# Query and key projections with 512-column products, adaLN slices in other places, filler products in some waits

## The chip, the cores and the metric

The kernel runs on one core of one Trainium2 chip. The metric is the device time of one execution in microseconds (us), here the median of three timed runs: 604.17 us (602.7 to 604.27). One further execution was recorded by the hardware profiler, and all rows below come from it.

## The reference

One layer of a decoder block in float32 on x of 256 rows (tokens) by 1024 channels, with a conditioning vector c:

```python
mod = silu(c) @ ada_w + ada_b                      # six rows of 1024: shift, scale, gate; twice
u = modulate(rms_norm(x, norm_mix_g), sh_a, sc_a)
proj = u @ w_in                                    # q_m k_m v_m o_m if_m | q_a k_a v_a | g_m g_a
...                                                # mLSTM on q_m k_m v_m; windowed attention on q_a k_a v_a (12 heads of 128)
y = sigmoid(g_m) * (h_m @ w_branch_m) + sigmoid(g_a) * (h_a @ w_branch_a)
x = x + gt_a * (y @ w_out)
u = modulate(rms_norm(x, norm_ffn_g), sh_f, sc_f)
x = x + gt_f * moe(u, ...)                         # 16 experts, two per token
return rms_norm(x, final_norm_g)
```

w_in alone is 1024 by 10760 numbers. q_a and k_a take 1536 of its columns each.

## The kernel before

**Precision.** Each weight tile and each activation is split into a high part in fp32r (a reduced float32 that TensorE multiplies in one pass) and a low part, the rest. A product of both is taken as three: high weight by high u, high weight by low u, low weight by high u, all summed in one PSUM bank (L1573 to L1577, L1595 to L1599).

**Blocks.** The projection weights are cut into groups of 512 columns (`GROUP_LIST`): four `qk`, two `vm`, three `qa` (groups 6 to 8), three `ka` (9 to 11), three `va` (12 to 14), two `o`, two `gm`, two `ga`, then the branch and output projections (`bm`, `ba`, `wo`). A block is half a group: 512 of the 1024 rows of its weights, 1 MB. The `qa` and `ka` groups are blocks 12 to 23, in pairs: an even block begins a group, the odd one ends it. In a channel-major group (`qk`, `qa`, `ka`, gates, branches) the weights are the stationary operand: for each of 4 column tiles c and 4 row tiles k there are three products of 256 moving columns (the 256 tokens). In the other groups u is stationary and the weights stream, 512 columns at a time.

**Pipeline.** SP loads blocks into four `raw` tiles, in the order of `STREAM`, and starts a load when the item four places ahead of it in that order is used up. For block s, the loop of ScalarE (ACT) makes the high part of block s+2 (`split_hi`, L613, one copy of 128x2048), VectorE (DVE) makes its low part (`split_lo`, L953), and TensorE (PE) multiplies block s. Each engine takes its instructions in the order in which they are written.

**Banks.** A group sums in two banks, 0 and 1 or 2 and 3, in turn (`banks_of`). For `qa` and `ka` ACT copies both banks out in one go when the group's second block is done (L721), and the group after next waits for that (`evacuated`, before its first product).

**adaLN slices.** The four later rows of `mod` are summed on DVE from 16 slices of `ada_w` of 1 MB each (`ada`, L982), which go through the same `raw` tiles. `ADA_AT` says in which block's loop turn each stands: 12, 13, 14, 15, 17, 18, 19, 21, 22, 23, 25, 26, 27, 30, 33, 36. A slice stands behind that turn's `split_lo` and ahead of its attention work on DVE.

**Between the blocks** PE does the mLSTM (a score after blocks 14, 16, 18, 20, L1645 to L1649; the values after 15, 17, 19, 21, L1662; small transposes after 12 and 13) and the attention (scores after 28, 31, 34, 37, turns after 30, 33, 36, 39, values after 31, 34, 37, 40).

**mod_p.** Behind block 41 ACT copies two rows of `mod` into `mod_p` (L782) once all 16 slices are summed, with one event for both. PE turns the first row into columns behind block 42 and the second behind block 43 (L1718).

**Routing.** After the last projection PE makes the router logits, DVE ranks experts and tokens (`picked`, `rank0`), and builds `onehot` for both token tiles t (L1340), with one signal at the end. PE then gathers the rows of the first experts (L1776). ACT rounds these rows (`xg_hi`), DVE makes their low part (`xg_lo`, L1330). In waits of this part PE also starts the sums of the output (`start_sums`, L1750) and does one product whose result nobody reads (L1758).

**Experts.** Eight pairs of experts follow (L1788 gate and up, L1800 and L1810 down). Their weights come through a ring of 19 chunks of 1 MB; SP loads the next chunk when one is used (L469).

## Time and profile before

| | us |
|---|---|
| median of the timed runs | 604.17 (602.7, 604.17, 604.27) |
| the profiled execution | 600.97 |
| its span, first to last instruction | 599.1 |
| PE busy | 577.4 (96%) |
| DVE busy | 306.9 (51%) |
| ACT busy | 238.7 (40%) |
| granted TensorE clock, mean | 0.997 |

The page first gives the busy time of each engine, then 40 slices of the span (busy tenths of each engine, granted clock, DMA), then the chain of work that ended last: followed back from the end, at each step to what released it. A busy time is an average over stages; what a change in one stage is worth is read in that stage, from what the chain passes through. The span leaves 1.87 us of the profiled execution's own time around it.

### The profile page before, as it was taken

The page shows a single profiled execution, that of the slowest core. Times are in us where ns is not written, and L with a number is a line of the kernel's source. Part 1 is how long each engine was busy: PE and PEld are TensorE (multiplying, and loading weights), DVE is VectorE, ACT ScalarE, POOL GpSimd, SP SyncE. Part 2 cuts the span into 40 slices and gives each one's busy share as a digit, 9 for nine tenths or more (in the row PEclk, how much of TensorE's full clock was granted, in tenths as well). Part 3 has the DMA queues.
Part 4 walks back from the last instruction along what each step waited for, and adds up shares of the span by engine and source line. Part 5 has one row for each costly group of instructions (what it writes and reads, how often), then busy time and mean ns, then how long its engine had stood idle before and what let it go on. Part 6 is the DMA issues. An engine that isn't in the chain of part 4 may idle for free.

```text
span 599.1 us, 8462 instructions
## 1 busy us (share of the span) xinstructions
PE 577.4 (96%) x3563; PEld 423.3 (71%) x3563; DVE 306.9 (51%) x461; ACT 238.7 (40%) x330; POOL 9.0 (2%) x23
## 2 busy tenths in 40 slices
PE   3999999999999999999999999999999999999995
PEld 0789988999998888999999988533534444353432
DVE  0679976766568966677546683712212130221204
ACT  5617658444454545764683334701111020111113
POOL 3001000000000000000000000000000000000000
PEclk9999999999999999999999999999999999999998
DMA  8999664785859947636558989399999999999992
GB/s 309 387 332 323 212 206 140 282 287 209 287 209 341 328 170 279 220 107 237 198 217 318 416 341 357 154 378 423 421 419 422 423 421 419 422 421 422 421 382 78
DMA packets 51577, 184.78 MB, mean 308 GB/s; under 512 B 3649, under 2 KB 3761, under 8 KB 37713
## 3 DMA queue, kind: packets, MB, share of 16 engines
q1 hardware_dynamic: 50706, 183.53, 79.7%
q8 instruction: 29, 0.48, 0.3%
q10 hardware_dynamic: 704, 0.58, 0.3%
q0 software_dynamic: 128, 0.11, 0.1%
q14 instruction: 10, 0.08, 0.0%
HBM read 183.16 MB, written 1.05 MB: 307 GB/s over the span
## 4 chain that ended last, share of the span: by engine, by line
PE 90%; DVE 3%; ACT 3%; DMA 1%; issue 1%; SPq 0%; ACTq 0%; DVEq 0%
PE ps L1576 30%; PE ps L1788 18%; PE ps L1598 16%; PE ps L1800 8%; PE ps L1834 3%; PE ps L1776 2%; DMA first_ada<-in_ada_w_dram 1%; PE ps L1810 1%; PE ps L1683 1%; PE ps L1698 1%; PE ps L1662 1%; PE ps L1494 1%; PE ps L1827 1%; DVE lo L953 1%; PE ps L1587 1%
## 5 line engine op out<-in xcount | busy, mean ns | idle before, releaser
L953 DVE TENSOR_TENSOR lo<-raw,hi 128x2048 fp32r<-128x2048 f32 (+1 forms) x51 | 114.2, 2248 | 41.2 <-ACT hi L613 40.8
L1576 PE MATMUL ps<-u_hi,hi 128*128 128x256 f32 x416 | 120.3, 289 | 0.7 <-DVE lo L953 0.7
L1576 PE MATMUL ps<-u_lo,hi 128*128 128x256 f32 x416 | 117.9, 283 | 0.0
L1576 PE MATMUL ps<-u_hi,lo 128*128 128x256 f32 x416 | 117.9, 283 | 0.0
L1788 PE MATMUL ps<-ring,xe_t 128*64 128x512 f32 x512 | 111.7, 593 | 0.0
L613 ACT CAST hi<-raw 128x2048 fp32r<-128x2048 f32 x50 | 94.9, 1908 | 36.0 <-PE ps L1576 25.5
L1788 PEld LDWEIGHTS ps<-ring,xe_t 128*64 128x64 f32 x512 | 36.5, 137 | 71.7 <-issue 71.4
L1576 PEld LDWEIGHTS ps<-u_hi,hi 128*128 128x128 f32 x416 | 79.8, 192 | 2.1 <-DVE lo L953 1.1
L1576 PEld LDWEIGHTS ps<-u_lo,hi 128*128 128x128 f32 x416 | 79.9, 192 | 0.2
L1576 PEld LDWEIGHTS ps<-u_hi,lo 128*128 128x128 f32 x416 | 79.9, 192 | 0.0
L1800 PE MATMUL ps<-ring,he_t 128*64 128x512 f32 x224 | 49.6, 596 | 0.0
L1399 DVE SCALAR_TENSOR_TENSOR he<-ps,w_slot,sg 128x512 f32<-128x512 f32 x8 | 6.0, 750 | 82.6 <-PE ps L1788 82.6
L1598 PE MATMUL ps<-hi,u_hi 128*128 128x512 f32 x112 | 44.4, 396 | 0.0
L1598 PE MATMUL ps<-lo,u_hi 128*128 128x512 f32 x112 | 43.7, 390 | 0.0
L1598 PE MATMUL ps<-hi,u_lo 128*128 128x512 f32 x112 | 43.7, 390 | 0.0
L1381 DVE TENSOR_TENSOR y_e<-ps,mod 128x512 f32<-128x512 f32 x16 | 10.4, 687 | 54.5 <-PE ps L1800 47.8
L982 DVE SCALAR_TENSOR_TENSOR mod<-raw,cs,mod 128x2048 f32<-128x2048 f32 x16 | 37.5, 2346 | 0.0
L1800 PEld LDWEIGHTS ps<-ring,he_t 128*64 128x64 f32 x224 | 15.5, 137 | 30.2 <-issue 28.0
L867 ACT CAST y_hi_e<-y_e 128x512 fp32r<-128x512 f32 x16 | 9.8, 618 | 62.8 <-DVE y_e L1381 62.8
L861 ACT COPY he_t<-ps 128x512 f32<-128x512 f32 x8 | 4.7, 586 | 64.3 <-PE ps L1827 64.3
L1598 PEld LDWEIGHTS ps<-lo,u_hi 128*128 128x128 f32 x112 | 21.0, 188 | 4.5
L1598 PEld LDWEIGHTS ps<-hi,u_hi 128*128 128x128 f32 x112 | 21.1, 188 | 4.2
(334 smaller groups left out, 837.0 us busy)
## 6 DMA issues: line engine op xcount, KB each, us to landing
raw<-in_w_in_dram SPq DMA_DIRECT2D x41, 1024.0 KB, 5.2
ring<-in_w_gate_e_dram SPq DMA_DIRECT2D x32, 1024.0 KB, 17.4
ring<-in_w_up_e_dram SPq DMA_DIRECT2D x32, 1024.0 KB, 16.0
ring<-in_w_down_e_dram SPq DMA_DIRECT2D x28, 1024.0 KB, 16.0
raw<-in_ada_w_dram SPq DMA_DIRECT2D x16, 1024.0 KB, 5.3
first_ada<-in_ada_w_dram SPq DMA_DIRECT2D x16, 512.0 KB, 11.8
raw<-in_w_branch_m_dram SPq DMA_DIRECT2D x4, 1024.0 KB, 5.5
raw<-in_w_out_dram SPq DMA_DIRECT2D x4, 1024.0 KB, 6.1
```

The lines of the kernel that those rows point to most:

```text
L613: nc.scalar.copy(hi[b % RING][:], src[:]).then_inc(hi_ready, 1)
L867: nc.scalar.copy(y_hi_e[:, h * NB:(h + 1) * NB], y_e[:, h * NB:(h + 1) * NB]).then_inc(y_hi_ready, 1)
L953: ins = V.tensor_tensor(lo[b % RING][:, tiles, :], src[:, tiles, :], hi[b % RING][:, tiles, :].bitcast(F32), ALU.subtract)
L982: V.scalar_tensor_tensor(out=dst, in0=src[:].rearrange("p k n -> p (k n)"), scalar=cs[:, k:k + 1], in1=dst, op0=ALU.mult, op1=ALU.add).the ...
L1381: ins = V.tensor_tensor(y_e[:, h * NB:(h + 1) * NB], ps[6 + h][:], mod[:, 3, h * NB:(h + 1) * NB], ALU.mult)
L1399: V.scalar_tensor_tensor(out=he[:], in0=ps[5][:], scalar=w_slot[:, side:side + 1], in1=sg[:], op0=ALU.mult, op1=ALU.mult).then_inc(he_read ...
L1576: ins = mm(dst, w[:, k, cols], x[:, k0 + k, :], start=(first and c % 2 == 0 and k == 0 and n == 0), stop=(end and k == KB - 1 and n == 2), ...
L1598: ins = mm(ps[banks[t]][:], x[:, k0 + k, rows_t], w[:, k, :], start=(first and k == 0 and n == 0), stop=(end and k == KB - 1 and n == 2))
L1776: ins = mm(dst, x[:, t, kk * P:(kk + 1) * P], onehot[:, t, 0:cols], start=(part == 0 and kk % 2 == 0 and t == 0), stop=(part == 1 and t == ...
L1788: ins = mm(ps[bank][64 * s:64 * s + 64, :], xe_t[:, kk, col + s * SLOTS:col + (s + 1) * SLOTS], w[:, k, :], start=(kk == 0), stop=(kk == K ...
L1800: ins = mm(ps[6 + h][64 * s:64 * s + 64, :], he_t[:, kk, s * SLOTS:(s + 1) * SLOTS], w[:, k, h * NB:(h + 1) * NB], start=(kk == 0), stop=( ...
L1834: ins = mm(ps[2 * t + h][:], scat[side][:, t * P:(t + 1) * P], y[:, h * NB:(h + 1) * NB], start=False, stop=False, skip_group_check=True)
```

## The change

1. **`qa` and `ka`.** The high and low part of u become two halves of one tile (`u_both`). For each c and k one product of 512 moving columns (high weight by both parts of u) takes the place of two of 256; the sum with the low part lands in the right half of the bank. The third product (low weight by high u) is as before. Each column tile c has a bank of its own, so a group takes four banks (2, 3, 0, 1) and the next group the same four.
2. **Getting the result out.** For each pair of banks ACT copies the right halves to `q_a` or `k_a` (`copy_right`), and DVE adds the left halves (`add_halves`). In a group's last block, ACT's copies for the first pair stand ahead of its `split_hi`, those for the second pair behind it, and DVE's sums likewise around its `split_lo`. PE waits for a pair's sum before it writes that pair in the next group (`wide_free`).
3. **adaLN slices** in loop turns 12, 14, 16, 18, 20, 22, 25, 26, 27, 29, 30, 32, 33, 36, 38, 39. As places, 13, 15, 17, 19, 21 and 23 are given up and 16, 20, 29, 32, 38 and 39 are taken.
4. **`mod_p`** has an event for each of its rows, and PE waits for the row it needs.
5. **Filler products**: eight of 256 columns ahead of block 3, five of 256 ahead of the last transposes of the routing, four (instead of one) ahead of `picked`.
6. **Routing order**: `start_sums(0, 0)` goes ahead of the wait for the last logits; `onehot` gives a signal after its first tile, and the first four gather products take the tiles in that order.

```diff
-ADA_AT = {s: ADA_FIRST + i for i, s in enumerate([12, 13, 14, 15, 17, 18, 19, 21, 22, 23, 25, 26, 27, 30, 33, 36])}
+ADA_AT = {s: ADA_FIRST + i for i, s in enumerate([12, 14, 16, 18, 20, 22, 25, 26, 27, 29, 30, 32, 33, 36, 38, 39])}
...
+            def copy_right(g, pair):
+                for c in (2 * pair, 2 * pair + 1):
+                    ins = nc.scalar.copy(wide_out(g, c), ps[wide_banks(g)[c]][:, T:2 * T])
+                ins.then_inc(halved, 1)
             for s in range(NBLK):
+                g, _, _, end = BLOCKS[s]
+                if end and g in WIDE:
...
+                    act.wait_ge(pair_done, WIDE.index(g) + 1)
+                    copy_right(g, 0)
                 if s + AHEAD < NBLK and s + AHEAD != EARLY and s != LAST_BLOCK[24]:
                     split_hi(s + AHEAD)
+                if end and g in WIDE:
+                    act.wait_ge(block_done, s + 1)
+                    copy_right(g, 1)
...
                     for m in range(2):
-                        ins = nc.scalar.copy(dealt(mod_p[:, m, :]), nearby(mod[:, 1 + m, :]))
-                    event(ins, "mod_p")
+                        event(nc.scalar.copy(dealt(mod_p[:, m, :]), nearby(mod[:, 1 + m, :])), f"mod_p{m}")
...
+            def add_halves(g, pair):
+                dve.wait_ge(halved, 2 * WIDE.index(g) + pair + 1)
+                for c in (2 * pair, 2 * pair + 1):
+                    ins = V.tensor_tensor(wide_out(g, c), ps[wide_banks(g)[c]][:, 0:T], wide_out(g, c), ALU.add)
+                ins.then_inc(summed, 1)
...
+                if end and g in WIDE:
+                    add_halves(g, 0)
                 if s + AHEAD < NBLK and s not in (1, LAST_BLOCK[24]):
                     split_lo(s + AHEAD)
+                if end and g in WIDE:
+                    add_halves(g, 1)
...
-            ins.then_inc(onehot_ready, 1)
+                ins.then_inc(onehot_ready if t else onehot_first, 1)
...
+            def keep_busy(bank, count, left, right):
+                for _ in range(count):
+                    mm(ps[bank][:, 0:T], left, right, start=True, stop=True)
...
-                if first and g >= EARLY:
-                    evacuated(pe, g - EARLY if g < EARLY + 2 else g - 2)
+                if first and g >= EARLY and g not in WIDE:
+                    if g - 1 in WIDE:
+                        wide_free(pe, g - 1, 0)
+                    else:
+                        evacuated(pe, g - EARLY if g < EARLY + 2 else g - 2)
...
+                if s == EARLY:
+                    keep_busy(6, 8, u_hi[:, 0, 0:P], u_hi[:, 0, :])
...
+                elif g in WIDE:
+                    for c in range(4):
+                        bank = wide_banks(g)[c]
+                        if first and c % 2 == 0:
+                            if g - 1 in WIDE:
+                                wide_free(pe, g - 1, c // 2)
+                            else:
+                                evacuated(pe, g - 2 + c // 2)
+                        cols = slice(c * P, (c + 1) * P)
+                        for k in range(KB):
+                            mm(ps[bank][:].rearrange("p (a t) -> p a t", a=2), w_hi[:, k, cols], u_both[:, :, k0 + k, :],
+                               start=(first and k == 0), stop=False, skip_group_check=True)
+                            ins = mm(ps[bank][:, 0:T], w_lo[:, k, cols], u_hi[:, k0 + k, :], start=False,
+                                     stop=(end and k == KB - 1), skip_group_check=True)
+                        if end and c == 1:
+                            ins.then_inc(pair_done, 1)
...
-                    after(pe, "mod_p", "a_turned3")
                     m = FFN_COL_AT.index(s)
+                    after(pe, f"mod_p{m}", "a_turned3")
...
             event(logits(0, 1), "logits0")
+            keep_busy(1, 5, y_hi[:, 0, 0:P], y_hi[:, 0, :])
             after(pe, "x1_1_t1_0", "x1_1_t1_1")
...
             event(ins, "x1_turn1_t1")
+            start_sums(0, 0)
             after(pe, "x1_copied1_t1", "x1_turned1_t1")
             event(logits(1, 1), "logits1")
...
             evacuated(pe, 26)
-            start_sums(0, 0)
-            for _ in range(1):
-                mm(ps[3][:, 0:T], ident[:], mod[:, 0, 0:T], start=True, stop=True)
+            keep_busy(3, 4, ident[:], mod[:, 0, 0:T])
             after(pe, "picked")
...
             after(pe, "xg_hi0_0", "xg_hi1_0")
-            pe.wait_ge(onehot_ready, 1)
-            gather_part(0, 4 * SLOTS, 4, (0,))
+            for t in range(TT):
+                pe.wait_ge(onehot_ready if t else onehot_first, 1)
+                for kk in range(2):
+                    mm(ps[4][:, kk * T:(kk + 1) * T], xg_hi[:, t, kk * P:(kk + 1) * P], onehot[:, t, :],
+                       start=(kk == 0 and t == 0), stop=False, skip_group_check=True)
```

## Rows read from the trace of the kernel before

**Rows 1.** The page: busy us, share of the span and instructions of each engine.

```profile
PE 577.4 (96%) x3563; PEld 423.3 (71%) x3563; DVE 306.9 (51%) x461; ACT 238.7 (40%) x330; POOL 9.0 (2%) x23
```

**Rows 2.** Chain that ended last, in order of time: start us, us, what.

```profile
112.59 0.21 PE ps L1633 x2
...
142.49 5.75 PE ps L1576 x48
...
155.93 1.30 PE ps L1662 x6
...
212.68 10.93 PE ps L1598 x48
...
410.30 13.73 PE ps L1788 x64
```

**Rows 3.** Waits of the SP queue: in total, times, longest.

```profile
SPq L469 <- PE ps L1788: 69.0, 26, 13.3
```

**Rows 4.** Timeline of ACT, blocks 17 and 18: start, duration, operation, idle before.

```profile
136.80 1.89 ACT L613 CAST hi<-raw 128x2048 fp32r<-128x2048 f32 x1
...
142.58 0.38 ACT L744 COPY h_m<-ps 128x256 f32<-128x256 f32 x1
```

**Rows 5.** Timeline of DVE: blocks 17 and 18, and one row of the last projection.

```profile
138.72 2.29 DVE L953 TENSOR_TENSOR lo<-raw,hi 128x2048 fp32r<-128x2048 f32 x1 [1.23 <-ACT hi L613]
140.93 2.35 DVE L982 SCALAR_TENSOR_TENSOR mod<-raw,cs,mod 128x2048 f32<-128x2048 f32 x1
...
372.27 0.42 DVE L1135 TENSOR_TENSOR scratch<-ps,mod 128x256 f32<-128x256 f32 x1
```

**Rows 6.** Timeline of DVE during attention, first instructions behind blocks 31 and 40.

```profile
234.03 0.42 DVE L1228 SCALAR_TENSOR_TENSOR bias_a<-dist,masks 128x256 f32<-128x256 f32 x1 [3.53 <-PE ps L1698]
...
300.50 1.66 DVE L1255 SCALAR_TENSOR_TENSOR hm_lo<-ps,vec,hm_hi 128x256 fp32r<-128x256 f32 x4 [4.83 <-ACT hm_hi L772]
```

**Rows 7.** The page: DMA issues, KB each, median us to landing.

```profile
raw<-in_ada_w_dram SPq DMA_DIRECT2D x16, 1024.0 KB, 5.3
```

**Rows 8.** Timeline of PE: first product of block 3, and mod_p.

```profile
45.06 0.39 PE L1557 MATMUL ps<-u_hi,hi 128*128 128x256 f32 x1 [0.94 <-DVE u_lo L1030]
...
312.13 1.95 PE L1718 MATMUL ps<-ones,mod_p 128*128 128x1 f32 x16 [0.89 <-ACT mod_p L782]
```

**Rows 9.** Timeline of ACT: both copies of mod_p.

```profile
307.98 4.10 ACT L782 COPY mod_p<-mod 128x1024 f32<-128x1024 f32 x2
```

**Rows 10.** Timeline of all engines during the routing.

```profile
373.29 0.72 PE L1743 MATMUL ps<-ident,x_res 128*128 128x128 f32 x4 [0.41 <-DVE rt L1282]
...
374.60 1.06 PE L1530 MATMUL ps<-rw_scaled,x_res_t 128*128 128x16 f32 x8 [0.59 <-DVE x_res_t L1289]
...
374.86 1.28 ACT L830 ACT_TABLE_LOAD   x1
...
377.31 1.02 PE L1750 MATMUL ps<-x_res,ident 128*128 128x512 f32 x2
...
378.17 0.60 PE L1758 MATMUL ps<-mod,ident 128*128 128x256 f32 x2
...
379.05 1.15 DVE L1330 SCALAR_TENSOR_TENSOR xg_lo<-x_res,st,xg_hi 128x512 fp32r<-128x512 f32 x1
379.18 0.41 PE L1762 MATMUL ps<-rt,bias_a 128*128 128x32 f32 x2 [0.42 <-DVE rt L1322]
...
380.32 0.76 DVE L1340 TENSOR_TENSOR onehot<-bias_a,rt 128x256 fp32r<-128x256 f32 x2
...
381.08 1.13 DVE L1330 SCALAR_TENSOR_TENSOR xg_lo<-x_res,st,xg_hi 128x512 fp32r<-128x512 f32 x1
...
382.27 1.21 PE L1776 MATMUL ps<-onehot,xg_lo 128*128 128x256 f32 x8
```

**Rows 11.** Stretches: us, busy time by engine, granted clock, DMA share, GB/s.

```profile
374.00:382.00 8.00, 6.75 (x31) 4.10 (x31) 6.19 (x29) 7.48 (x10) 0.00 (x0) 1.00 0.74 309
...
595.00:599.10 4.10, 0.00 (x0) 0.00 (x0) 0.90 (x2) 0.72 (x1) 0.00 (x0) 0.56 0.68 256
```

More of the change, by code:

```diff
@@ L69 @@
 AHEAD = RING - 1
+WIDE = [_g for _g, (_kind, _, _) in enumerate(GROUP_LIST) if _kind in ("qa", "ka")]
 CONV_AT = {3: (0, 0), 4: (0, 1), 5: (1, 0), 6: (1, 1), 7: (2, 0), 8: (3, 0), 9: (3, 1), 10: (2, 1)}
@@ L158, in build @@
         lo = [at(f"lo{i}", 56 + 8 * i, [P, KB, NB], F32R) for i in range(RING)]
-        u_hi = at("u_hi", 80, [P, KT, T], F32R)
-        u_lo = at("u_lo", 88, [P, KT, T], F32R)
+        u_both = at("u_both", 80, [P, 2, KT, T], F32R)
+        u_hi, u_lo = u_both[:, 0], u_both[:, 1]
         hm_hi = at("hm_hi", 80, [P, KT, T], F32R)
@@ L281, in build @@
         xe_early = sem("xe_early")
+        onehot_first = sem("onehot_first")
         onehot_ready, slots_turned, gathered, xe_act, xe_dve, scat_ready, scattered = (sem(n) for n in (
@@ L348, in plan @@
                 if s == M_TURN_AT[1]:
-                    act += ["ha_hi", "mod_p"]; dve.append("ha_lo")
+                    act += ["ha_hi", "mod_p0", "mod_p1"]; dve.append("ha_lo")
                 if s == FFN_COL_AT[1]:
@@ L400, in evac_engine @@
         def evac_engine(g):
+            if GROUP_LIST[g][0] in ("qa", "ka"):
+                return "sums"
             return "dve" if GROUP_LIST[g][0] in ("qk", "bm", "ba", "wo") else "act"
@@ L406, in banks_of, with wide_banks, wide_out, wide_free @@
             return 2 * n, 2 * n + 1
+        def wide_banks(g):
+            return 2, 3, 0, 1
+        def wide_out(g, c):
+            kind = GROUP_LIST[g][0]
+            j = [x for x in WIDE if GROUP_LIST[x][0] == kind].index(g)
+            return {"qa": q_a, "ka": k_a}[kind][:, 4 * j + c, :]
+        def wide_free(eng, g, pair):
+            eng.wait_ge(summed, 2 * WIDE.index(g) + pair + 1)
         def evacuated(eng, g):
+            if g in WIDE:
+                wide_free(eng, g, 1)
+                return
             e = evac_engine(g)
@@ L706, in _ @@
                         after(act, "m_val3")
-                    if kind == "qa" and j == 0:
-                        after(act, "u_lo1_3")
                     if kind == "va" and j == 0:
                         after(act, "m_val3")
-                    dst = {"va": v_a, "o": sig_o, "qa": q_a, "ka": k_a, "gm": sig_gm, "ga": sig_ga}.get(kind)
+                    dst = {"va": v_a, "o": sig_o, "gm": sig_gm, "ga": sig_ga}.get(kind)
                     for n, bank in enumerate(banks):
@@ L1046, in _ @@
             ada(4)
+            def add_halves(g, pair):
[3 more added lines that the diff above has]
+                ins.then_inc(summed, 1)
             for s in range(NBLK):
+                g, _, _, end = BLOCKS[s]
+                if end and g in WIDE:
+                    add_halves(g, 0)
                 if s + AHEAD < NBLK and s not in (1, LAST_BLOCK[24]):
                     split_lo(s + AHEAD)
+                if end and g in WIDE:
+                    add_halves(g, 1)
                 if s == 0:
@@ L1744, in _, with start_sums @@
             event(ins, "x1_turn1_t1")
+            def start_sums(t, h):
+                mm(ps[2 * t + h][:], ident[:], x_res[:, t, h * NB:(h + 1) * NB], start=True, stop=False, skip_group_check=True)
+            start_sums(0, 0)
             after(pe, "x1_copied1_t1", "x1_turned1_t1")
             event(logits(1, 1), "logits1")
-            def start_sums(t, h):
-                mm(ps[2 * t + h][:], ident[:], x_res[:, t, h * NB:(h + 1) * NB], start=True, stop=False, skip_group_check=True)
             for n in range(2):
```

3 lines of the change are left out of this document (added).

## The prediction

> **What bounds the kernel now.** I read the busy times first: PE is busy for 577.4 of 599.1 us and no other engine for more than 51% [rows 1]. Such a share doesn't say that PE sets the time in every stage, so I read the chain of waits next. The reader should see that in the blocks it runs from PE product to PE product without a gap [rows 2], that it leaves PE only around mod_p (0.89 us of waiting [rows 8]) and in the routing (waits of 0.41, 0.59 and 0.42 us [rows 10]), and that the experts are again PE alone. The SP queue's waits come third: the experts' loads wait for PE (69.0 us for L1788 alone [rows 3]), so a start of the experts that is earlier by some time brings their loads forward by the same time. What PE saves ahead of the experts should therefore arrive whole at the end; a transfer doesn't swallow it. Last come ACT and DVE in the same blocks, because the change gives them more to do between two products.
>
> **Part 1, the products.** 48 products of 256 columns take 5.75 us, so 0.1198 us each; 48 of 512 take 10.93 us, so 0.2277 each [rows 2]. Twice the columns cost 0.108 us more, so some 0.012 us of each product doesn't depend on its columns. Before, one column tile c and row tile k cost 3 x 0.1198 = 0.3594 us; after it costs 0.2277 + 0.1198 = 0.3475, which is 0.0119 less. There are 12 blocks x 16 of them, 192, so -2.3 us, all of it PE time on the chain. No row shows a product whose moving columns come as two strips of 256, nor the two lengths in turn, so I bound it: if the strips cost what two products cost, the gain is 0 (a loss would need a strip dearer than a product of its own, for which no row speaks); if 512 columns cost as little as in the experts' products (13.73 us for 64, 0.2145 each [rows 2]) and 256 half of that, a tile costs 0.322 and the gain is 7.2 us. I take 2.3, since the rows with the same kind of number and the same stationary size give it.
>
> By the Trainium skill (TensorE: Matmul & The Clock Gate, Back-to-back issue gap) a product costs its columns at 2.4 GHz plus 2.5 ns, so joining two saves only 2.5 ns, an estimated 0.5 us over 192. The rows show about 12 ns, so I go by the rows; the rule's outcome is a rival below.
>
> **Part 1, getting results out.** A wide block takes 16 x 0.3475 = 5.56 us. Call its start B. The first pair of banks is done at B+2.78. ACT then copies two halves: 0.38 us each [rows 4], so about B+3.5; DVE adds two, 0.42 each for this size [rows 5], so about B+4.3. PE needs that pair at the next group's start, B+5.56 or later: 1.2 us to spare. Queued behind ACT's wait for the pair are its split of block s+2 (1.89 us [rows 4]) and everything after it; it now ends at about B+5.4, and DVE's low part (2.29 us [rows 5]) at B+7.7. PE wants that low part a whole block and more later, so no cost. Then the second pair: copied at about B+6.3, but its sums stand behind DVE's low part, so B+8.5. PE wants this pair in the middle of the next group's first block: B+5.56, plus the work between the blocks, plus 2.78. That work is 1.30 us for the values behind blocks 15, 17, 19 and 21 [rows 2], so B+9.6 and 1.1 us to spare; behind block 13 it is only 0.21 us [rows 2], so B+8.55 and nothing to spare. Behind block 23 no wide group follows, and group 12 needs the first pair at once, when DVE and ACT have just done the mLSTM's scale: another place with little cover. I take 0.2 us for both, bounds 0 and 2. The old copies of `qa` and `ka` and their waits go at no gain: the chain holds no wait for them.
>
> **Part 3, the slices.** The six places given up are exactly the turns with the new sums. That takes 6 x 2.3 = 14 us off DVE there and the two new places, 16 and 20, put 4.6 back; six of the ten slices of this stretch stay, all in even turns. If all ten had stayed, one slice of 2.35 us [rows 5] would stand ahead of several second-pair sums that have 1.1 us or less to spare. So this move gains nothing by itself; it pays for part 1. The four taken later (29, 32, 38, 39) fall on DVE time during the attention: DVE idles 3.53 us ahead of its work on the scores of block 31 (block 34's is alike, of the two rows one stands), and 4.83 us ahead of the turns of block 40 [rows 6]. One slice of 2.27 us of queue fits in each of the first two; 38 and 39 together, 4.5 us, fit in the last. Each also brings its load on the SP queue: 1 MB that lands after 5.3 us [rows 7], in one of four tiles, so the weight block behind it is asked for one item later and ACT may get it 2 to 3 us later than before. PE wants a block about two blocks (11 us) after its load, so this is covered. The cost is 0; if that cover is gone, one slice, 2.3 us, at one place.
>
> **Part 4.** mod_p's two copies run from 307.98 for 4.10 us [rows 9]; the first ends at about 310.0. PE starts on the first row at 312.13 after 0.89 us of waiting [rows 8], so it was free at 311.24. With an event for each row it goes on at once, and the second row is ready long before block 43 ends: -0.9 us, bounds -1.0 and 0. The last slice, now in turn 39, falls into DVE's idle time that ends at 300.50 [rows 6], ahead of 307.98.
>
> **Part 5, filler products.** Ahead of block 3 PE waits 0.94 us [rows 8]; eight products of 0.12 us fill it: 0, at most +0.1. Five ahead of the last transposes (0.6 us) fill a wait of 0.41 [rows 10]: up to +0.2. Four ahead of `picked`: `start_sums(0, 0)`, which took 0.86 us of PE's queue (377.31 to 378.17), leaves this place, and three more products come; one of 256 columns in float32 takes 0.60 us to its end alone and about half of the 0.86 of one of 512 in a row, 0.43. So +0.4 us against a wait of 0.42 [rows 10]: 0 to +0.2. The granted clock is 1.00 through the routing [rows 11], so in this execution there is nothing to win with them.
>
> **Part 6.** `start_sums(0, 0)` takes 0.86 us in a wait of 0.59, so the last logits come 0.3 us later; the sigmoid after them waits for ACT's table load anyway (374.86 to 376.14 [rows 10]), which hides 0.2 of it. The split signal lets PE gather 0.38 us earlier (half of 0.76), but the low-part products start at 382.27, and DVE's second low part ends at 382.21 [rows 10]: the time is lost in the next wait. Parts 5 and 6 together: +0.1, bounds -0.2 and +0.6.
>
> **The sum.** -2.3 + 0.2 - 0.9 + 0.1 = -2.9 us. The profiled execution took 600.97 us, so 598.1 in its terms. The timed runs took 602.7 to 604.27, 1.7 to 3.3 us more than the profiled one, which no row explains; I carry the difference over unchanged: 604.17 - 2.9 = 601.3 us, 0.5% less. A measurement of this kernel can tell about 0.3% (1.8 us) from no change.
>
> **The rivals.**
>
> *The joined product saves nothing.* Two strips cost what two products cost. For it: no row shows strips. Against: both lengths carry the same 12 to 14 ns. Part 4 alone is left: 604.17 - 0.9 + 0.3 = about 603.6. By the Trainium skill's rule above it would be 603.1, an estimate, within this rival's reach and part of its chance.
>
> *Waits take the gain.* The new bank waits cost 0.4 us at each of five borders between wide groups: -2.9 + 2.0, 603.3. For it: one set of four banks instead of two in turn, and no spare time behind block 13. Against: 1.1 us at four borders.
>
> *Slower: DVE becomes the bound in blocks 12 to 23.* Its queue holds split, slice, mLSTM score and four sums for each group; if its second-pair sums come 2.7 us later than counted (one slice or split more ahead of them), PE waits 1.6 us at four borders and 2.7 at one: +9.1, so about 610. It decides from 1.9 us of lateness on, where the waits (4 x 0.8 + 1.9 = 5.1) pass 2.9 + 1.8 and the 0.2 counted. Against: DVE idles here, 1.23 us ahead of one split [rows 5].
>
> *The filler products win what the profile can't show.* The clock does fall when PE has nothing to do: 0.56 granted in the last 4.1 us [rows 11], that is 1.2 GHz for most of it. If the 1.7 to 3.3 us by which the timed runs are longer are such stretches in the waits that are now filled, they go too: 598 to 599.6. The Trainium skill (TensorE: Matmul & The Clock Gate, Part 1) says that the slow clock is the default and activity releases it. The trace agrees at its end, and shows no fall in the waits concerned.
>
> **How the numbers follow.** Forecast 0.58, products save nothing 0.07, waits take the gain 0.13, slower 0.08, filler products win 0.14. The forecast's own bounds are 600.0 to 602.6, so most but not all of it counts as faster. Faster: 0.50 of the forecast, and 0.14: 0.64. Within 0.3%: the rest of the forecast, both middle rivals: 0.28. Slower: 0.08. The range leaves out the slower rival and the far half of the last one: 598.7 to 603.7.
>
> **What would show it.** Right: PE blocks 12 to 23 at about 5.56 us each with 16 products of 512 and 16 of 256; no PE wait for DVE's sums over 0.2 us; no wait ahead of L1718; the routing within 0.3 us of 373.3 to 382.3 in length; the same pitch in the experts. Wrong: a tile of 0.36 us for the first rival; PE waits named after the add lines at each border for the second and third; a fall of the granted clock somewhere in a profile for the last. The forecast fails most easily where DVE's order in the odd turns is later than I counted.

## The result

| | before | after |
|---|---|---|
| timed runs, median (range) | 604.16 us (602.7 to 604.27, 4 runs) | 597.67 us (597.18 to 598.16, 4 runs) |
| ratio after/before, 95% interval | | 0.9906 [0.9881, 0.9931] |
| profiled execution: time, span | 600.97, 599.1 | 597.18, 595.4 |
| start of the first block's products | 23.08 | 22.43 |
| first of the gates' running sums, ahead of block 12 | 100.05 | 99.39 |
| start of block 24 | 183.32 | 180.61 |
| start of the `mod_p` products | 312.13 | 308.40 |
| start of the experts' products | 384.37 | 380.62 |

The change gained 6.5 us; I had predicted 2.9. The two profiled executions differ by 3.7 to 3.8 us only. So two things are to be explained: the 3.7, and the other 2.8.

**The 3.7 us between the traces.** The table's differences from row to row are what each stage gained: 0.65 before the first block, in work that the change doesn't touch; 2.05 in blocks 12 to 23; 1.05 around `mod_p` (312.13 to 308.40 is 3.73 earlier, block 24 was 2.71 earlier, and the stages between lost 0.03); after that nothing, for the start of the experts is 3.75 earlier and the end 3.7. The 0.65 are scatter and no gain: in the fourteen traces without idle products at the start (those of the experiments below among them) the first block starts at 22.10 to 23.22 us, early or late with either kernel (22.21 in e3, which is the kernel before but for eight products; 23.22 in e14, which is nearly the kernel after). So some 3.1 us are the change's. First the busy times of after, from the page, for [rows 1]:

```profile
PE 577.1 (97%) x3390; PEld 414.3 (70%) x3390; DVE 315.2 (53%) x485; ACT 240.3 (40%) x342; POOL 9.0 (2%) x23
```

PE's busy sum hardly moved (577.4 before), since the idle products (the filler products of the change) count as busy; a sum over the span would have hidden both gains. Then the chain that ended last (start us, us, what), whose rows answer [rows 2, 8]:

```profile
119.19 0.45 PE ps L1721 x4
125.18 1.30 PE ps L1734 x6
...
180.77 27.24 PE ps L1670 x120
...
302.81 5.76 PE ps L1648 x48
308.56 1.68 PE ps L1790 x16
```

Block 15 begins at 119.19 + 0.45 = 119.64 and ends at 125.18: 5.54 us where a block took 5.75. `mod_p` (L1790, the old L1718) follows the block before it without a gap. And two column-and-row tiles of the new form, in PE's timeline of after:

```profile
123.97 0.40 PE L1625 MATMUL ps<-u_both,hi 128*128 128x512 f32 x1
124.20 0.28 PE L1627 MATMUL ps<-u_both,lo 128*128 128x256 f32 x1
124.32 0.39 PE L1625 MATMUL ps<-u_both,hi 128*128 128x512 f32 x1
124.55 0.27 PE L1627 MATMUL ps<-u_both,lo 128*128 128x256 f32 x1
124.67 0.40 PE L1625 MATMUL ps<-u_both,hi 128*128 128x512 f32 x1
```

From 123.97 to 124.67 two tiles: 0.35 each, where the sum had 0.3475. Between 100 and 184 us the trace of after lists no wait of PE. The loads of the experts wait for PE as before (waits of the SP queue, for [rows 3]):

```profile
SPq L491 <- PE ps L1860: 70.3, 26, 13.4
```

In the routing the timeline of PE, for [rows 10], has the idle products where waits were, and the one wait that is left stands where the sum had put it, ahead of the low-part products:

```profile
368.90 0.84 PE L1576 MATMUL ps<-y_hi 128*128 128x256 f32 x5
369.58 0.65 PE L1816 MATMUL ps<-ident,x_res 128*128 128x128 f32 x4
370.06 1.02 PE L1820 MATMUL ps<-x_res,ident 128*128 128x512 f32 x2
...
378.52 1.22 PE L1848 MATMUL ps<-onehot,xg_lo 128*128 128x256 f32 x8 [0.17 <-DVE xg_lo L1376]
```

**The other 2.8 us** are not in these two traces. The expectations below go by two theories. The one is that part of before's executions lose granted TensorE clock behind short waits (a fall, below: a stretch at a granted clock of 0.50), which the idle products and the halved `mod_p` take away. The rival is that products, slices and `mod_p` are worth more than the traces show, or that the chips and moments differ.

### The profile page after: what moved, and what is told of

It reads as the page before. It is cut to its first block, busy times and chain, and to the rows that moved or that the text cites. A ratio compares the mean times of both kernels' runs of the same rounds, so it can differ in the third digit from the quotient of the medians.

```text
span 595.4 us, 8152 instructions
## 1 busy us (share of the span) xinstructions
PE 577.1 (97%) x3390; PEld 414.3 (70%) x3390; DVE 315.2 (53%) x485; ACT 240.3 (40%) x342; POOL 9.0 (2%) x23
## 3 DMA queue, kind: packets, MB, share of 16 engines
HBM read 183.16 MB, written 1.05 MB: 309 GB/s over the span
## 4 chain that ended last, share of the span: by engine, by line
PE 92%; DVE 3%; ACT 2%; DMA 1%; issue 1%; SPq 0%; ACTq 0%; DVEq 0%
PE ps L1648 20%; PE ps L1860 19%; PE ps L1670 16%; PE ps L1872 8%; PE ps L1625 8%; PE ps L1627 4%; PE ps L1906 3%; PE ps L1848 2%; DMA first_ada<-in_ada_w_dram 1%; PE ps L1882 1%; PE ps L1659 1%; PE ps L1770 1%; PE ps L1755 1%; PE ps L1734 1%; PE ps L1540 1%; PE ps L1899 1%
## 5 line engine op out<-in xcount | busy, mean ns | idle before, releaser
L1648 PE MATMUL ps<-u_both,hi 128*128 128x256 f32 x448 | 82.1, 285 | 0.7 <-DVE lo L987 0.7
L1648 PEld LDWEIGHTS ps<-u_both,hi 128*128 128x128 f32 x448 | 69.8, 191 | 2.1 <-DVE lo L987 1.1
L1670 PE MATMUL ps<-hi,u_both 128*128 128x512 f32 x224 | 69.8, 393 | 0.0
L1625 PE MATMUL ps<-u_both,hi 128*128 128x512 f32 x192 | 68.8, 401 | 0.0
L1648 PE MATMUL ps<-u_both,lo 128*128 128x256 f32 x224 | 63.4, 283 | 0.0
L1627 PE MATMUL ps<-u_both,lo 128*128 128x256 f32 x192 | 53.7, 279 | 0.0
L1670 PEld LDWEIGHTS ps<-hi,u_both 128*128 128x128 f32 x224 | 41.7, 188 | 8.5
L1670 PE MATMUL ps<-lo,u_both 128*128 128x512 f32 x112 | 43.7, 390 | 0.0
L1648 PEld LDWEIGHTS ps<-u_both,lo 128*128 128x128 f32 x224 | 42.9, 191 | 0.0
L1625 PEld LDWEIGHTS ps<-u_both,hi 128*128 128x128 f32 x192 | 36.0, 188 | 8.0
L1627 PEld LDWEIGHTS ps<-u_both,lo 128*128 128x128 f32 x192 | 36.2, 189 | 0.1
```

The costliest lines, as they stand in the source:

```text
L1625: mm(ps[bank][:].rearrange("p (a t) -> p a t", a=2), w_hi[:, k, cols], u_both[:, :, k0 + k, :], start=(first and k == 0), stop=False, skip ...
L1627: ins = mm(ps[bank][:, 0:T], w_lo[:, k, cols], u_hi[:, k0 + k, :], start=False, stop=(end and k == KB - 1), skip_group_check=True)
L1648: ins = mm(dst, w[:, k, cols], x[:, k0 + k, :], start=(first and c % 2 == 0 and k == 0 and n == 0), stop=(end and k == KB - 1 and n == 2), ...
L1670: ins = mm(ps[banks[t]][:], x[:, k0 + k, rows_t], w[:, k, :], start=(first and k == 0 and n == 0), stop=(end and k == KB - 1 and n == 2))
```

## The experiments

Each was timed beside the kernel before on its own chip. "Clock" is the mean granted clock of an execution; before's trace has 0.997 without any fall but that of the last microseconds, where PE has no work [rows 11].

**The kernel before, seen often.** The experiments below hold 81 further executions of it, in five sets on four chips. By their mean clock they come in three groups:

| mean clock | executions | median us | range |
|---|---|---|---|
| 0.995 to 0.997 | 44 | 601.3 | 600.7 to 601.7 |
| 0.991 to 0.992 | 27 | 602.8 | 602.5 to 603.2 |
| 0.987 to 0.990 | 10 | 604.5 | 604.2 to 606.1 |

The profiled execution (600.97) belongs to the first group; of the four by which the change was judged, by their times, three lie at 604.2, in the last, and one in the second. That was an unusual draw: the last group holds 10 of the 81, and the median of all 81 is 601.5 us, so that after (597.6 over ten executions) is 3.9 us below it, and not 6.5. The two slower groups make up from 3 of 13 to 9 of 17 executions, by set; whether the sets differ by chance or by something of the chip isn't shown. None of the ten executions of after (597.0 to 598.4) has a clock below 0.996.

The mean clock also holds the end of the span, where PE has no work: there the traces stand at 0.50 for 1.5 to 4.6 us, which costs nothing and takes 0.001 to 0.004 off the mean. Between 0.995 and 0.997 it therefore doesn't tell whether there was a fall: e2's and e8's traces, at 0.995, hold one behind a wait, after's, at 0.996, none. The first group isn't shown to be free of falls; the 37 executions at 0.992 or less lost more than the end accounts for in any trace.

**Without the idle products.**

```diff
# kernel after
-                if s == EARLY:
-                    keep_busy(6, 8, u_hi[:, 0, 0:P], u_hi[:, 0, :])
...
-            keep_busy(1, 5, y_hi[:, 0, 0:P], y_hi[:, 0, :])
...
-            keep_busy(3, 4, ident[:], mod[:, 0, 0:T])
+            keep_busy(3, 1, ident[:], mod[:, 0, 0:T])
```

> The changed kernel without the filler products (none ahead of block 3 and of the last transposes, one ahead of picked as before). Theory A (the fillers keep TensorE's clock from falling in runs that the one profile of before doesn't show): about 600.5 us, that is 597.7 plus most of the 1.7 to 3.3 us by which the timed runs of before were longer than its profiled one. Theory B (the products, mod_p and the order make the whole gain, the fillers nothing): 597.7 within 0.4. Either way blocks 12 to 23 gain 2.05 us and the wait ahead of mod_p is gone.

Measured: 598.37 us (596.89 to 599.07, 6 runs), ratio to before 0.9945 [0.9928, 0.9962]; its trace has no fall ahead of the last microseconds and a span of 595.1. The time lies between the two theories: most of the gain stands without idle products, and they are worth at most about 0.8 us here.

**Idle products and the moved `start_sums` on the kernel before.**

```diff
# kernel before
+                if s == EARLY:
+                    keep_busy(6, 8, u_hi[:, 0, 0:P], u_hi[:, 0, :])
...
+            keep_busy(1, 5, y_hi[:, 0, 0:P], y_hi[:, 0, :])
...
+            start_sums(0, 0)
             after(pe, "x1_copied1_t1", "x1_turned1_t1")
...
-            start_sums(0, 0)
-            for _ in range(1):
-                mm(ps[3][:, 0:T], ident[:], mod[:, 0, 0:T], start=True, stop=True)
+            keep_busy(3, 4, ident[:], mod[:, 0, 0:T])
```

> The kernel before with the filler products alone and the earlier start_sums(0, 0) that makes room for them. Theory A: about 601 us (604.2 less 1.7 to 3.3), close to the profiled 600.97. Theory B: 604.2 within 0.4, perhaps 0.1 to 0.2 longer.

Measured: 601.76 us (600.82 to 602.77, 12 runs), ratio 0.9994 [0.9977, 1.0011]. The executions with a clock of 0.992 or less are gone. The median is 0.9 us below that of the 23 executions of before beside it (602.67), but the interval of the ratio holds no change, and the lowest times (600.82 and 600.72) are the same. The trace shows why there is no more: a fall in a place that no idle product covers. Stretches, with the columns of [rows 11]:

```profile
313.60:317.60 4.00, 4.00 (x23) 4.00 (x22) 4.00 (x2) 1.31 (x1) 0.00 (x0) 0.57 0.38 81
374.00:382.00 8.00, 7.74 (x37) 4.89 (x36) 5.51 (x31) 7.34 (x12) 0.00 (x0) 1.00 0.81 316
```

This is block 43, right behind the wait for `mod_p` and its sixteen one-column products: 23 products in 4 us, where the trace of before has 35 from 314 to 318. The routing is at full clock.

**Only the eight early ones; only `start_sums`.** e3 is before with the first of these edits, e4 with the third:

```diff
# e3
+                if s == EARLY:
+                    keep_busy(6, 8, u_hi[:, 0, 0:P], u_hi[:, 0, :])
# e4
+            start_sums(0, 0)
             after(pe, "x1_copied1_t1", "x1_turned1_t1")
...
-            start_sums(0, 0)
```

> The kernel before with the eight fillers ahead of block 3 alone. Theory A if the clock falls there: about 601 us. Theory A if it falls in the routing: 604.2. Theory B: 604.2.

> The kernel before with start_sums(0, 0) moved ahead of the wait for the last logits, and nothing else. In the runs so far 12 of 23 executions of before had a mean granted clock of 0.992 or less and spans of 601 to 604 us, the others 0.995 to 0.997 and 599.0 to 599.7; with all late fillers none of 12 fell. Theory A1 (filling the wait of 0.59 us is enough to keep the clock): no execution at 0.992 or less, median about 601.2 us. Theory A2 (the filler products are needed): about half of the executions at 0.992 or less, median 602 to 603. Its own price: 0 to +0.2 us.

Measured: e3 603.27 us (600.85 to 604.67), ratio 1.0015 [0.9997, 1.0032]; e4 603.70 us (601.12 to 604.97), ratio 1.0021 [1.0005, 1.0037]; 12 runs each. Neither holds the clock: eight of e3's executions stand at 0.992 or less, and eleven of e4's, though e4 moves only 0.86 us of work. The traces name the places. The stretches of e4:

```profile
45.00:50.00 5.00, 5.00 (x31) 5.00 (x31) 4.90 (x10) 5.00 (x6) 1.65 (x3) 0.66 0.99 312
314.80:318.40 3.60, 3.60 (x20) 3.60 (x19) 3.60 (x2) 1.45 (x1) 0.00 (x0) 0.53 0.39 88
382.80:386.40 3.60, 3.35 (x15) 3.13 (x15) 3.60 (x8) 1.22 (x2) 0.00 (x0) 0.54 0.00 0
```

Three places: block 3 behind its wait of 0.94 us, block 43 behind `mod_p`'s, the gather behind the routing's waits. In e4's timeline of PE one sees the pitch of the products of 256 columns double:

```profile
312.70 1.95 PE L1718 MATMUL ps<-ones,mod_p 128*128 128x1 f32 x16 [0.89 <-ACT mod_p L782]
...
314.71 0.33 PE L1576 MATMUL ps<-hm_lo,hi 128*128 128x256 f32 x1
314.84 0.41 PE L1576 MATMUL ps<-hm_hi,lo 128*128 128x256 f32 x1
315.06 0.42 PE L1576 MATMUL ps<-hm_hi,hi 128*128 128x256 f32 x1
315.27 0.41 PE L1576 MATMUL ps<-hm_lo,hi 128*128 128x256 f32 x1
```

0.21 us from start to start instead of 0.12: 1.2 instead of 2.4 GHz. Against the trace of before, this stage (first `mod_p` product to first product of the last projection) took 35.89 instead of 34.39 us, so a fall here costs 1.5 us. In e3's trace block 3 is at full clock, and two falls are left: one behind `mod_p`, whose stage takes 35.88 us, and one of 7 us in the routing, which takes 20.23 instead of 17.60. They account for the whole time: 599.1 (the span of before's trace), less 0.87 for a first block that starts at 22.21, plus 1.5 and 2.6 is 602.3, and e3's span is 602.4.

**After, without idle products and with `start_sums` in its old place.**

```diff
# e1, and
-            start_sums(0, 0)
             after(pe, "x1_copied1_t1", "x1_turned1_t1")
...
             evacuated(pe, 26)
+            start_sums(0, 0)
```

> The changed kernel with the routing's waits as before: no filler products, start_sums(0, 0) in its old place with one filler. Theory A1 or A2 (it is the work in these waits that keeps the clock): about half of the executions at a granted clock of 0.992 or less, times of 597, 599 and 600.5 us, median some 1.5 us over the changed kernel's 597.7. Theory A3 (the clock is kept by the earlier end of the blocks, not by these waits): none falls, median about 597.3.

Measured: 598.84 us (597.97 to 599.74, 6 runs), ratio 0.9949 [0.9934, 0.9964]. The falls are back in two of the three places (45 to 48.6 at 0.55, 372.8 to 376.4 at 0.53 in its trace, span 598.0), and not behind `mod_p`, whose halves this kernel keeps.

**The old slices in after.**

```diff
# kernel after
-ADA_AT = {... [12, 14, 16, 18, 20, 22, 25, 26, 27, 29, 30, 32, 33, 36, 38, 39])}
+ADA_AT = {... [12, 13, 14, 15, 17, 18, 19, 21, 22, 23, 25, 26, 27, 30, 33, 36])}
```

> The changed kernel with the adaLN slices where they were before (10 in blocks 12 to 23, none in 16, 20, 29, 32, 38, 39). My step on the slices: the second-pair sums come late, PE waits 1 to 2 us more in all at the borders of the wide groups, so 598.7 to 599.7 us, and blocks 12 to 23 keep 0 to 1 us of their gain. Rival (DVE had room for all): 597.7 within 0.4, and no PE wait for the sums.

Measured: 598.37 us (598.0 to 599.2, 6 runs), a little below the expected 598.7 to 599.7, ratio 0.9945 [0.9931, 0.9958], at a clock of 0.998 or 0.999. Blocks 12 to 23 take 82.36 us in its trace, 1.14 more than in after; the waits of PE between 100 and 184 us (total, times, longest) show part of it, and after shows none:

```profile
PE ps L1625 <- DVE q_a L1086: 0.4, 1, 0.4
PE ps L1734 <- DVE turned L1251: 0.2, 1, 0.2
```

So the slices' move gains by itself what the old order would have cost the new sums: 1.1 of the 2.05 us, of which 0.6 is in waits that the view names.

**Everything but the new products and slices.** e2 with `mod_p` in two halves.

```diff
# e2, and
-                        ins = nc.scalar.copy(dealt(mod_p[:, m, :]), nearby(mod[:, 1 + m, :]))
-                    event(ins, "mod_p")
+                        event(nc.scalar.copy(dealt(mod_p[:, m, :]), nearby(mod[:, 1 + m, :])), f"mod_p{m}")
...
-                    after(pe, "mod_p", "a_turned3")
+                    after(pe, f"mod_p{m}", "a_turned3")
```

> The kernel before with all idle products, start_sums in its new place and mod_p in two halves; products and slices stay old. By the theory that three places lose granted clock in part of the executions, and that the two halves of mod_p mend the one behind the modulation (about 313 to 318 us), no place is left: 600.8 (the best executions of e2) less 1.05 for the shorter wait is 599.7, with every execution within 0.8 us of it, median 599.7 to 600.2. Kernel after less this one is then what products and slices are worth, 2.0 to 2.5 us. Rival: the fall behind the modulation does not hang on the length of that wait; then part of the executions still lose 1.5 us there, the median is 600.6 or more and the spread is over 1.5 us.

Measured: 599.49 us (598.76 to 600.43, 6 runs), ratio 0.9957 [0.9944, 0.9971], no fall in the trace ahead of the last microseconds and every execution at 0.997 or 0.998. This is the first theory's outcome, with small misses: the median is 0.2 us under its range, one execution 0.9 from 599.7, and the spread of 1.7 us would fit the rival; but the rival's median (600.6 or more) and its fall are not there. After (597.6 over ten executions) is 1.9 us below this, for products and slices, where 2.0 to 2.5 were expected.

**`mod_p` in two halves, alone on the kernel before:** the edit just shown, without e2.

> The kernel before with mod_p in two halves and nothing else. By the theory of three places every execution gains 1.05 us, and those that lost 1.5 us behind the modulation gain that too; the falls at 45 to 50 us and in the routing stay in part of the executions: best executions at 599.5 to 600.2, median 600.0 to 601.5, a profile that shows no fall from 310 to 320 us. Rival: that fall stays; then its profile or a group of executions 1.5 us longer shows it, and the median is 1.0 us below before's and no more.

Measured: 600.74 us (598.77 to 602.75, 12 runs), ratio 0.9966 [0.9943, 0.9988]. The twelve lie in three bunches: 598.8 to 599.0, 600.3 to 601.1, 602.4 to 602.8. The lowest lies under the range expected for it (599.5 to 600.2) and 2.4 us under the first group of before on the same chip (601.1 to 601.6), though the halves gain 1.06 us in the trace (from block 24 to `mod_p` it takes 127.75 us, in before's 128.81). An execution of before with a first block at 22.10 and no fall would have a span of 599.1 - 0.98 = 598.1, and the shortest of the 81 has 599.0; so that first group seems to lose about 1 us more to late starts or to falls of its own, and which it is no trace shows. e13's trace:

```profile
309.00:317.00 8.00, 8.00 (x70) 8.00 (x69) 4.09 (x3) 6.68 (x4) 0.00 (x0) 1.00 0.76 304
373.60:380.40 6.80, 6.80 (x15) 3.70 (x16) 3.91 (x22) 5.43 (x8) 0.00 (x0) 0.50 0.82 325
```

No fall behind `mod_p`, a long one in the routing. What that costs, in its timeline of PE (the four products of `mod` by ones took 1.96 us in the trace of before):

```profile
373.44 1.70 PE L1529 MATMUL ps<-rw_scaled,x_res_t 128*128 128x16 f32 x8 [0.59 <-DVE x_res_t L1288]
374.98 3.76 PE L1752 MATMUL ps<-mod,ones 128*128 128x512 f32 x4
378.53 1.92 PE L1749 MATMUL ps<-x_res,ident 128*128 128x512 f32 x2
```

The routing, from the first product of the logits to the first of the experts, takes 20.26 us in this trace and 17.60 in that of before: 2.7 us for one fall. The shorter one of e5 makes it 18.59 against 17.68 in after, 0.9, and that of e4 18.90 against 17.60, 1.3.

**Which idle products matter.** Each is after less one or two of its idle products:

```diff
# e8
-                if s == EARLY:
-                    keep_busy(6, 8, u_hi[:, 0, 0:P], u_hi[:, 0, :])
# e9, e14
-            keep_busy(1, 5, y_hi[:, 0, 0:P], y_hi[:, 0, :])
# e14
-            keep_busy(3, 4, ident[:], mod[:, 0, 0:T])
+            keep_busy(3, 1, ident[:], mod[:, 0, 0:T])
```

> The kernel after without the eight idle products ahead of block 3. By the theory of three places, the stretch from 45 to 50 us falls to half the clock in part of the executions, which adds 0.9 us to those: 597.2 to 599, median 597.5 to 598.5, with two groups of spans. Rival: the fall of e4 and e5 at 45 to 50 us came with start_sums in its old or lone place, or by chance, and not from this wait; then all executions stand as those of after, and eight products of 1 us in all cost or save nothing over 0.2 us.

> The kernel after without the five idle products on the attention output in the routing (the four on the scratch bank and the eight early ones stay). If these five hold the clock through the routing, part of the executions fall to half the clock somewhere from 368 to 385 us, which adds 1 to 2.6 us: some of 599 or more. Rival: the four ahead of the experts, or start_sums in its new place, are enough: all executions within 0.6 us of after.

> The kernel after with only the eight early idle products (none in the routing but the one that the kernel before had). e1, without any, was 0.7 us above after, and e8, without the eight alone, 0.7 too. If the eight early ones are all that pays, this is after again: 597.2 to 598.2, no execution below a clock of 0.995. Rival: the late ones hold the clock in the routing: part of the executions lose 1 us or more there, some of 599 or more.

Measured: e8 598.38 us (598.0 to 598.8, 5 runs), ratio 0.9940 [0.9926, 0.9955]; e9 597.77 (597.09 to 598.18, 6 runs), 0.9932 [0.9919, 0.9945]; e14 597.13 (596.92 to 598.83, 6 runs), 0.9912 [0.9886, 0.9938]. e8's trace has the fall ahead of the value blocks:

```profile
45.00:48.60 3.60, 3.60 (x20) 3.60 (x20) 3.50 (x9) 3.60 (x6) 1.65 (x3) 0.55 1.08 383
```

From the first product of block 0 to the first of L1670 (512 columns) it takes 52.35 us, after 51.48: 0.87 us. Of its five executions that one alone stands at 0.995, though; the other four, at 0.997, are between 596.3 and 596.8 in span, with no trace. And e1's trace, without the eight too, has the wait of 0.94 us ahead of block 3 and no fall: it takes 51.48 us, as after. e9 and e14 show no fall in their traces and stand with after, but for one execution of e14 at 598.83. So in the kernel after, with `start_sums` moved and `mod_p` halved, the idle products in the routing buy nothing that these runs show; the eight early ones cost nothing, and the fall that costs 0.9 us was seen there only without them (e4, e5, e8), in part of the executions.

**After once more.** The same kernel as after.

> The kernel after itself once more, beside more executions of the kernel before on the same chip. The kernel before took 601.5 to 602.7 us in the larger sets of e1 to e10 and 604.2 in the two small sets by which the change was judged. If that gap is the share of executions of before that lose granted clock, after stays at 597.2 to 598.2 with a clock of 0.995 or more each time, and the difference lies between 3.5 us (against executions of before without a fall) and 6.5 us. Rival: the chips or the moments differ; then after moves with before, by 2 us or more.

Measured: 597.53 us (597.02 to 598.36, 6 runs); before on the same chip 602.61 (601.08 to 605.94, 17 runs); ratio 0.9916 [0.9891, 0.9941]. After stayed where it was, before spread over its three groups. The difference, 5.1 us, lies in the first theory's 3.5 to 6.5, and after didn't move with before, as the rival had it.

**Idle products at the start.** The 0.65 us before the first block lie in products of the same work: sixteen transposes took 2.46 us in before and 1.97 in after, and the first eight products 1.94 in both where later ones take 1.06. Such slow products at the start come and go from execution to execution (in the trace of e14, whose edit lies in the routing, the transposes take 2.74). e10 adds fourteen idle products of 128 columns at the very start of after, e12 eighteen; e15 adds twenty-four, and five between the first two groups; e16 is e15 with e14's edit.

```diff
# kernel after (e15)
+            for _ in range(24):
+                mm(ps[1][:, 0:P], ident[:], ident[:], start=True, stop=True)
             pe.wait_ge(rows_loaded, 80)
...
                 row_sums(0, 2, a, a == 0, False)
+                if a == 0:
+                    for _ in range(5):
+                        mm(ps[1][:, 0:P], ident[:], ident[:], start=True, stop=True)
```

> The kernel after with fourteen more idle products, of 128 columns, at the very start, where the matrix engine has nothing to do for 9.7 us and its first products then take 1.94 us for eight where the same form later takes half. If these first products are slow because the granted clock is still low, and idle products raise it sooner, the stage up to the first block (start at 22.4 us) is 0.3 to 0.9 us shorter: median 596.7 to 597.4. Rival: the chain there is set by the input's transfers, which land at about 12 us, or the clock comes up no sooner: within 0.2 us of after.

> Like e10, with eighteen instead of fourteen idle products at the start, so that the matrix engine is busy to about 9.5 us and goes on without the idle 2.1 us behind which e10 fell to half the clock. If that idle time made the fall, the first eight products take about 1.06 us instead of 1.93 and the first block starts 0.3 to 0.8 us earlier than at 22.1 to 22.4: median 596.9 to 597.5. Rival: the products run past 9.7 us and hold the real ones up, or the input's landing at about 12 us sets the stage: 597.5 to 599.

> The kernel after with twenty-four idle products of 128 columns at the start and five between the first two groups on first_ada, in the 1.24 us of idle time behind which e12 fell to half the clock. By the theory that it is such idle time, the second group takes 1.06 us instead of 1.94 and the sixteen transposes behind it 1.97 at most instead of up to 2.67: first block at 20.9 to 21.6 us instead of 22.1 to 23.2, median 596.2 to 597.0, with a narrower spread. Rival: the transfers of the input, which run without a break from 5 us on, set the stage; then the waits grow by what the products lose, and it is 597 to 598.5.

> e14 with the same products at the start as e15: the version that by the theories of e14 and e15 does best, 595.9 to 596.8. If the idle products in the routing are needed after all, some executions are 1 us or more above the others; if the transfers set the start, it is e14 again, 596.9 to 598.8.

Measured: e10 599.15 us (597.46 to 599.49), 0.9954 [0.9940, 0.9968]; e12 598.01 (596.96 to 598.34), 0.9917 [0.9892, 0.9942]; e15 599.03 (598.09 to 600.55), 0.9955 [0.9935, 0.9975]; e16 597.97 (596.95 to 600.51), 0.9935 [0.9913, 0.9956]. None is better than after, and each trace shows the same reason at another place. In e12's timeline of PE the first group now takes 1.06 us, then waits for a load and runs the next at half the clock:

```profile
9.93 1.06 PE L1540 MATMUL ps<-first_ada,cs 128*32 128x512 f32 x8
12.24 1.94 PE L1540 MATMUL ps<-first_ada,cs 128*32 128x512 f32 x8 [1.24 <-DMA first_ada<-in_ada_w_dram]
14.10 2.67 PE L1563 MATMUL ps<-ident,x_in 128*128 128x128 f32 x16
```

In e15's that wait is filled, the transposes take 1.96 us, and the wait reappears ahead of the fourth group:

```profile
12.34 1.06 PE L1540 MATMUL ps<-first_ada,cs 128*32 128x512 f32 x8
13.34 1.96 PE L1566 MATMUL ps<-ident,x_in 128*128 128x128 f32 x16
...
18.62 1.06 PE L1540 MATMUL ps<-first_ada,cs 128*32 128x512 f32 x8 [1.26 <-DMA first_ada<-in_ada_w_dram]
```

Behind it the granted clock is 0.50 from 20.4 to 27.2 us, and the first block starts at 25.1 instead of 22.4. The stage is bounded by its loads (386 to 389 GB/s from 3 to 27 us); being early only makes the idle time longer, and the clock falls behind it.

## Why the prediction was wrong

**The products: right.** Tile 0.347 us against 0.3475; blocks 12 to 23 gained 2.05 us in the trace, with 2.3 - 0.2 = 2.1 predicted. The rule of the Trainium skill (TensorE: Matmul & The Clock Gate, Back-to-back issue gap), which it gives for a product by itself and by which joining two saves 2.5 ns, would have given an estimated tile of 0.357; the trace decides against it, at 0.347, for these products in a row, each with its own weights. The first rival falls with the tile of 0.347.

**Results, waits, slices: right.** No PE wait for DVE's sums, so the second and third rival fall. That the old slices would have cost time is what e6 measured, 1.1 us, 0.6 of it in waits that its trace names; I had said so without a number.

**`mod_p`: right in the trace, too small in the timed runs.** 0.9 predicted, 1.05 in the trace. But the wait was also the start of a fall of the clock in part of the executions, 1.5 us each (the traces of e2, e3 and e4 have it, those of e5, e7 and e13 with the halves do not). That price is missing in the sum.

**Idle products and routing: right for an execution without falls** (0.1 predicted; the routing stage of after is within 0.1 us of before's). "In this execution there is nothing to win with them" was right, and the words "in this execution" were what mattered.

**The step that failed: "I carry the difference over unchanged".** In the profile's own terms the sum gave 598.1 us; the profiled execution of after took 597.18; with the 0.65 that its earlier start happened to save it is 597.8, against 598.1. The forecast's error is the 1.7 to 3.3 us that the timed runs of before lay above its profiled one. I took them for a fixed offset of timed against profiled runs. What the runs showed in its place are falls of the granted clock to half behind short waits, at 0.9 to 2.7 us each in the traces of kernels one small edit away; in the kernel before itself at least 37 of 81 executions (0.992 or less in the mean, 602.5 to 606.1 us) are read as having them. The change takes away the places where they begin: the wait for `mod_p` at 312 us by the halves, the wait ahead of block 3 by the eight idle products, those of the routing by its new order. So after's timed runs lie 0 to 1.0 us above its profiled one (597.18, itself the lowest of the four), and not 1.7 to 3.3. The sum that fits is 604.17 - 2.9 - 3.2 = 598.1, which is the number in the profile's own terms. How far the forecast missed is in part the draw: from the median of the 81 executions, 601.5, the same -2.9 gives 598.6, 1.0 us above the 597.6 of after.

I had this as the rival "The filler products win what the profile can't show" and gave it 0.14, since no row of before shows a fall in the waits concerned. Its time, 598 to 599.6, was the nearest, and its mechanism right in the main, though the idle products are only one of three things that remove the falls, and most of the gain stands without them (e1, 598.37). What spoke for it stood in the same table: a profiled execution 0.3 to 0.5% faster than every timed run is no offset but a sample of another kind. A fixed offset would have needed a reason, and I had none.

**What stays open.** For the kernel before itself no trace holds a fall; that its longer executions fall in the same three places is inferred from kernels that differ from it by one small edit (e3, e4, e13) and from its mean clocks. What keeps the clock in the routing isn't told apart either: in the kernel after the moved `start_sums` was enough without the late idle products (e1, e14), in the kernel before it alone was not (e4), and the late idle products without the moved `start_sums` were not run. Why one execution falls behind a wait and the next does not, no row shows. And e8's four executions without a trace lie 1.1 to 1.6 us above the shortest span of after (595.2); the start of the first block alone scatters by 1.1 us between traces, but whether that is the reason isn't shown.

## What to carry to other kernels

Where the timed runs of a kernel lie above its profiled one, look at the mean granted clock of each run before taking the gap for an offset: groups of runs like those here at 0.997, 0.992 and 0.990 point to waits that cost the clock in some executions, and an edit of such a wait is worth its length plus the fall's price times its share. And take many executions of the kernel before: of the four here three were of its slowest group, and 3.9 us looked like 6.5. Shorten the wait first (`mod_p` in halves) and fill what can't be shortened. Where a load bounds a stage, don't bring TensorE's work forward into it.

## What the runs showed of the hardware

- Behind waits of 0.6 to 1.5 us (2.1 in e10) the granted clock fell to 0.50 for 3.4 to 7 us, in some traces and not in others. The length of the wait doesn't decide it: behind 0.94 us ahead of block 3 the clock fell in e4, e5 and e8 and not in before and e1, and behind 1.27 us ahead of `picked` in e4 and not in e1 (1.27 too) and e14 (1.26). A fall costs 0.9 us in the stage of block 3, 1.5 in a stretch of products (block 43), 0.9, 1.3 and 2.6 to 2.7 in the routing.
- Small edits move its place and its share: with 0.86 us of work moved (e4) 11 of 12 executions stood at 0.992 or less, beside 8 of 17 of before.
- The granted clock column stands at 1.00 from 9 to 14 us in the traces of before and after, while the products there take 1.94 us for eight that take 1.06 later. There the column doesn't tell the clock; the durations do.
- A moving operand in two strips of 256 columns, half a tile apart, costs what one strip of 512 costs (0.228 us within a tile of 0.347).
